# A hybrid decoder layer on one core: new homes for merged values, attention gates, turned merged tile and biases, and an earlier place in the queue for two expert half-matrices

## The chip, the cores and the metric

One core of a Trainium2 chip runs the whole layer as one program. The metric is the device time of the program in microseconds (us). The core has a matrix engine (PE, with its weight loads shown apart as PEld), a vector engine (DVE), a scalar engine (ACT), GpSimd (POOL), and SyncE (SP), which here only issues transfers. Sixteen DMA engines carry the transfers of all queues; SP's queue is q1 in the profile, POOL's is q0.

## The reference, cut to what matters

```python
# mixer: all from one input projection of the normalised x
o = diff_attention(q, k, v, lam)                   # branch A, 8 heads
y_attn = (rmsnorm(o, g_subln) * 0.8) @ w_b_attn
y_pool = multiscale_pool(u_pool, ...) @ w_b_pool   # branch B
y_mem = memory_cross_attention(...) @ w_b_mem      # branch C
g = sigmoid(gate_logits + b_gates)                 # three gates of 1024 channels
merged = g[0] * y_attn + g[1] * y_pool + g[2] * y_mem
h = x + merged @ w_out
# channel sub-layer: top 4 of 32 experts, 256 tokens, widths 1024
logits = rmsnorm(h) @ w_router + b_router
for e in experts:                                  # 12 MB of float32 weights each
    g = min(xb @ w_gate[e] + b_gate[e], 7); u = clip(xb @ w_up[e] + b_up[e], -7, 7)
    out = (g * sigmoid(1.702 * g) * (u + 1)) @ w_down[e] + b_down[e]
    y[rows] += out * weights
```

## The kernel before

**The mixer.** All mixer weights are cut into 22 pieces (`PIECES`), each loaded in two halves of 1 MB. `load(H)` issues half H on SP's queue into buffer `raw[H % 5]` once half H-5 has been used. ACT makes its high part (`hi`, L693), DVE the low part (`lo_whole`, L973), and PE multiplies (`unit`, L1483, 24 matmuls of 128x512 in a unit, or 12 for the pool and memory branches). Units are numbered: 20 to 23 are the pool branch's gates, 24 to 27 that branch, 28 to 35 the memory branch, 36 to 39 the attention gates (`ga0`, `ga1`), 40 to 43 the attention branch's product (`wba0`, `wba1`), 44 to 47 the output projection (`wo0`, `wo1`). Unit u writes PSUM bank u % 3, so unit u + 3 waits until DVE has read it. While units 21 to 36 run, PE interleaves the attention heads between them: for head h the turned q and k (`turn_qk`, semaphore `qk_done`), the scores, the turned probabilities, the values (`values`, L1626 to L1628, semaphore `pv_done`) and the turned output (`turn_o`, L1637, semaphore `oT_done`).

**Gates.** For a gate unit DVE adds the bias (`add_bias`, L1166), which POOL's queue has loaded as a broadcast 512 KB tile for each of two token tiles (`gate_bias`, L615), and ACT applies a tanh (`gate_exp`, L704). `merge` (L1185, L1190) multiplies each branch by its gate and sums into `MG`; the semaphore `merged` counts the sums, four of them for the memory branch. After the last sum PE turns `MG`, ACT and DVE split it into `MGT` high and low, and units 44 to 47 use it.

**Routing.** `add_h` (L1277) adds the projection to x. PE turns h (L1688), computes logits (L1693), DVE routes (L1291 to L1307, L1333, L1351), PE dispatches tokens (L1701), and the experts begin (L1773).

**The experts.** 16 pairs of experts, each with 12 half-matrices of 2 MB ("halves" below; 24 MB for a pair). They stream on SP's queue through a ring of 10 places of 2 MB. Half g goes to place g % 10. The ring lies over the mixer's buffers: place 0 over the attention scratch, 1 over `region9` and `mem_low`, 2 over `x_low` and `region7`, 3 over `hi4` and `raw4`, 4 over `region2` and `region8`, 5 to 8 over the other `hi` and `raw` buffers, 9 over `region1` and `region10`. So each of the first ten halves can only be issued when its place's mixer tenants are dead. SP issues in the order of its program; a wait in that program holds back all that stands behind it. Halves 10 to 17 are issued in quarters of 1 MB as PE uses up the first places (L550, L553), later ones in pieces of 2 or 4 MB.

```python
buffers = ("region9", "mem_low", "x_low", "region7", "hi4", "raw4", "region2", "region8", ...,
           "hi3", "raw3", "region1", "region10", "region0", "region5", "region3", "region4", "region6")
G = {"p": rows(6, "t"), "m": rows(7, "t"), "a": rows(6, "t")};  MG = rows(8, "t")
MGT = (rows_r(10), rows_r(1), None)
```

So `MG` sits in place 4, `MGT` in place 9, and the attention gates take the room of the pool gates.

## Time and profile before

| what | us |
|---|---|
| median of 3 runs (1213.93 to 1214.83) | 1213.95 |
| the profiled execution | 1214.63 |
| its span in the trace | 1212.8 |
| PE busy / DVE busy / ACT busy / POOL busy | 1169.5 / 436.5 / 260.5 / 43.7 |
| first expert matmul (L1773) | at 302.39 |
| granted PE clock, mean | 0.99 |

A row of the trace gives a start, a duration, the engine, the source line, the operation and its operands, and, in brackets, the idle time before it with what ended it. Transfers show two times: the issue on the queue, and the time from issue to landing.

### The profile page before, as it was taken

To read this page: it belongs to the slowest core of one execution; us is meant where nothing else is said; L and a number is where in the kernel's file an instruction comes from. 1 tells how busy PE (TensorE), PEld (TensorE's weight loads), DVE (VectorE), ACT (ScalarE), POOL (GpSimd) and SP (SyncE) were. 2 spreads that over 40 slices of the span, in tenths; PEclk is the share of its full clock that TensorE was granted. 3 is DMA by queue.
4 is the path that set the end of the run, shared out by engine and by line. 5 is a ranking of instruction groups with operands and counts; after the bars stand their busy time and mean duration, and the time that the engine had idled before them with its cause. 6 is when DMAs were issued, how large, how long until landed. Compare 5 with 4: busy or idle time off the path is not lost.

```text
span 1212.8 us, 13717 instructions
## 1 busy us (share of the span) xinstructions
PE 1169.5 (96%) x5436; PEld 581.0 (48%) x5436; DVE 436.5 (36%) x758; ACT 260.5 (21%) x463; POOL 43.7 (4%) x72
## 2 busy tenths in 40 slices
PE   9999999999999999999999999989898989899998
PEld 5888888888434344342434343433333343433342
DVE  5788798665222222222222121212122222221222
ACT  5655477542110110111010001101010101010101
POOL 1321101100000000000000000000000000000000
PEclk9999999999999999999999999999999999999999
DMA  9745645689999999999999999999999999999995
GB/s 384 267 148 185 214 142 186 224 363 394 406 427 431 427 432 432 431 432 431 430 431 430 429 429 432 431 432 431 431 431 432 432 432 431 431 431 431 425 428 232
DMA packets 28172, 460.67 MB, mean 380 GB/s; under 512 B 3216, under 2 KB 3984, under 8 KB 6608
## 3 DMA queue, kind: packets, MB, share of 16 engines
q1 hardware_dynamic: 27008, 456.34, 89.4%
q0 software_dynamic: 960, 3.41, 0.9%
q8 instruction: 49, 0.80, 0.3%
q14 instruction: 11, 0.09, 0.0%
q10 hardware_dynamic: 144, 0.03, 0.0%
HBM read 458.72 MB, written 1.05 MB: 379 GB/s over the span
## 4 chain that ended last, share of the span: by engine, by line
PE 66%; DMA 32%; issue 1%; DVE 1%; POOL 0%; SPq 0%; DVEq 0%; POOLq 0%
DMA experts_ring<-in_w_up 32%; PE bank L1773 25%; PE bank L1483 19%; PE bank L1818 7%; PE bank L1701 5%; PE bank L1761 2%; PE bank L1783 2%; PE bank L1447 1%; PE bank L1476 1%; PE bank L1784 1%; DMA raw<-in_mixer_halves 0%; PE bank L1847 0%; PE bank L1693 0%; PE bank L1602 0%; PE bank L1798 0%
## 5 line engine op out<-in xcount | busy, mean ns | idle before, releaser
L1773 PE MATMUL bank<-experts_ring,region 128*64 128x512 f32 x2048 | 468.4, 608 | 31.9 <-DMA experts_ring<-in_w_gate 21.2
L1773 PEld LDWEIGHTS bank<-experts_ring,region 128*64 128x64 f32 x2048 | 150.2, 139 | 325.5 <-issue 317.5
L1818 PE MATMUL bank<-experts_ring,region 128*64 128x512 f32 x1024 | 228.7, 596 | 2.1 <-DMA experts_ring<-in_w_down 1.9
L1483 PE MATMUL bank<-hi_split,region_split 128*128 128x512 f32 x400 | 151.3, 401 | 0.0
L1818 PEld LDWEIGHTS bank<-experts_ring,region 128*64 128x64 f32 x1024 | 73.6, 137 | 137.6 <-issue 136.4
L1483 PE MATMUL bank<-raw_split,region_split 128*128 128x512 f32 x336 | 130.9, 389 | 0.0
L944 ACT ACTIVATE region<-region 128x512 f32<-128x512 f32 x32 | 20.1, 629 | 452.3 <-DVE region L1409 452.3
L973 DVE TENSOR_TENSOR raw_split<-raw,hi_split 128x2048 fp32r<-128x2048 f32 x42 | 96.1, 2288 | 33.9 <-ACT hi_split L693 33.7
L1417 DVE TENSOR_SCALAR region<-bank 128x512 f32<-128x512 f32 x32 | 22.1, 692 | 236.7 <-PE bank L1784 236.7
L1409 DVE TENSOR_SCALAR region<-bank 128x512 f32<-128x512 f32 x32 | 22.1, 691 | 226.3 <-PE bank L1784 226.3
L1483 PEld LDWEIGHTS bank<-hi_split,region_split 128*128 128x128 f32 x400 | 75.1, 188 | 17.4 <-issue 2.6
L693 ACT ACTIVATE hi_split<-raw 128x2048 fp32r<-128x2048 f32 x42 | 80.1, 1912 | 14.7 <-DMA raw<-in_mixer_halves 14.7
L1432 DVE COPY region<-bank 64x512 f32<-64x512 f32 x32 | 22.2, 694 | 168.7 <-PE bank L1818 168.7
L1483 PE MATMUL bank<-hi_split,x_low_split 128*128 128x512 f32 x208 | 81.2, 390 | 0.0
L1483 PEld LDWEIGHTS bank<-raw_split,region_split 128*128 128x128 f32 x336 | 63.2, 188 | 12.4 <-issue 0.2
L1701 PEld LDWEIGHTS bank<-region 128*128 128x128 f32 x544 | 63.4, 192 | 2.0 <-DVE region L1333 0.5
L1701 PE MATMUL bank<-region 128*128 128x128 f32 x544 | 63.8, 275 | 0.4 <-DVE region L1333 0.4
L1761 PE MATMUL bank<-region 128*128 128x512 f32 x128 | 61.9, 606 | 0.0
L956 ACT ACTIVATE region<-bank 64x512 f32<-64x512 f32 x32 | 18.9, 590 | 152.3 <-PE bank L1818 152.3
L1392 DVE TENSOR_TENSOR region<-bank,region 128x512 f32<-128x512 f32 x68 | 43.9, 685 | 2.4 <-PE bank L1847 2.4
L1483 PEld LDWEIGHTS bank<-hi_split,x_low_split 128*128 128x128 f32 x208 | 39.0, 188 | 8.5
L1783 PEld LDWEIGHTS bank<-extra_split,region_split 128*128 128x128 f32 x64 | 11.9, 186 | 51.9 <-issue 51.9
(183 smaller groups left out, 760.2 us busy)
## 6 DMA issues: line engine op xcount, KB each, us to landing
experts_ring<-in_w_gate SPq DMA_DIRECT2D x26, 4096.0 KB, 36.6
experts_ring<-in_w_up SPq DMA_DIRECT2D x26, 4096.0 KB, 38.8
experts_ring<-in_w_down SPq DMA_DIRECT2D x26, 4096.0 KB, 39.2
raw<-in_mixer_halves SPq DMA_DIRECT2D x44, 1024.0 KB, 5.0
experts_ring<-in_w_up SPq DMA_DIRECT2D x10, 2048.0 KB, 11.1
experts_ring<-in_w_down SPq DMA_DIRECT2D x9, 2048.0 KB, 14.2
experts_ring<-in_w_gate SPq DMA_DIRECT2D x8, 2048.0 KB, 23.3
experts_ring<-in_w_gate SPq DMA_DIRECT2D x8, 1024.0 KB, 9.3
```

What stands on the lines that cost most here:

```text
L693: nc.scalar.activation(upper(H), raw(H), ACT.Copy).then_inc(hi_act, 1)
L973: nc.vector.tensor_tensor(lower(H), raw(H), upper(H), ALU.subtract).then_inc(lo_ready, 1)
L1392: nc.vector.tensor_tensor(X[:, t, h * HALF:(h + 1) * HALF], bank[banks[j]][:, :], X[:, t, h * HALF:(h + 1) * HALF], ALU.add).then_inc(y_ad ...
L1409: nc.vector.tensor_scalar(GS, bank[0][:, :], LIMIT, None, ALU.min).then_inc(g_read, 1)
L1417: nc.vector.tensor_scalar(US, bank[1][:, :], LIMIT, -LIMIT, ALU.min, ALU.max).then_inc(u_read, 1)
L1432: nc.vector.tensor_copy(OE[e * SLOTS:(e + 1) * SLOTS, HALF:D], bank[(2, 1)[e]][SLOTS:2 * SLOTS, :]).then_inc(o_hi, 1)
L1483: ins = nc.tensor.matmul(unit_bank(u)[:, :], a[:, k, toks], b[:, cols], start=(k == 0 and m == 0), stop=(k == k_n - 1 and m == 2))
L1701: ins = nc.tensor.matmul(bank[4 + half][:, b * P:(b + 1) * P], rows_[:, t, (4 * half + b) * P:(4 * half + b + 1) * P], PT[:, t, :], start= ...
L1761: nc.tensor.matmul(bank[6 + j % 2][:, :], PWT[:, t * P:(t + 1) * P], OE[:, h * HALF:(h + 1) * HALF], start=True, stop=True).then_inc(comb_ ...
L1773: ins = nc.tensor.matmul(dst[h * SLOTS:(h + 1) * SLOTS, :], XE[:, kk, e * SLOTS:(e + 1) * SLOTS], w[:, k, h * HALF:(h + 1) * HALF], start= ...
L1783: nc.tensor.matmul(dst[:, :], pick, BIAS_UP, start=False, stop=False)
L1818: ins = nc.tensor.matmul(bank[(2, 1)[e]][h * SLOTS:(h + 1) * SLOTS, :], AHT[e][:, k, half * SLOTS:(half + 1) * SLOTS], w[:, k, h * HALF:(h ...
```

## The change

Regions are given out anew. `MG` moves from `region8` to `region6` (the pool gates' own place, each value overwritten by its product); the attention gates move from `region6` to `region4`, where V is; `MGT` moves from `region10` and `region1` to `region4` and `region6`, laid out by token tile; the low part of the turned attention output moves from `region2` to `region3`, whose K is laid out by halves; `region1` and `region7` swap ring places; the expert biases go into `con`; the turned h goes to `region5`. With that, places 4 and 9 have no tenant after the last scores and the memory merge, and SP issues halves 4 and 9 there. Since V must be dead first, the attention gates' bias is now loaded after the last head's values. The router's weights and `b_down` are loaded later.

```diff
-        buffers = ("region9", "mem_low", "x_low", "region7", "hi4", "raw4", "region2", "region8", "hi0", "raw0",
-                   "hi1", "raw1", "hi2", "raw2", "hi3", "raw3", "region1", "region10",
+        buffers = ("region9", "mem_low", "x_low", "region1", "hi4", "raw4", "region2", "region8", "hi0", "raw0",
+                   "hi1", "raw1", "hi2", "raw2", "hi3", "raw3", "region7", "region10",
...
-        G = {"p": rows(6, "t"), "m": rows(7, "t"), "a": rows(6, "t")}
-        MG = rows(8, "t")
+        G = {"p": rows(6, "t"), "m": rows(7, "t"), "a": rows(4, "t")}
+        MG = rows(6, "t")
...
-        MGT = (rows_r(10), rows_r(1), None)
+        MGT = tuple(region_r[i][:, :].rearrange("p (t k n) -> p t k n", t=NT, k=KD) for i in (4, 6))
...
             for H in range(HALVES + 1, 2 * N0):
-                if H == 2 * PIECES.index("wba0") + 1:
+                load(H)
+                if H == 2 * PIECES.index("ga1"):
+                    sp.wait_ge(qk_done, HEADS)
+                    load_half(0, 4)
+                if H == 2 * PIECES.index("wba0"):
+                    sp.wait_ge(merged, 4)
+                    load_half(0, 9)
                     sp.wait_ge(pv_done, HEADS)
                     biases()
-                    sp.wait_ge(merged, 4)
                     load_half(0, 0)
-                load(H)
-                if H == 2 * PIECES.index("wba1") + 1:
+                if H == 2 * PIECES.index("wba1"):
                     sp.wait_ge(oT_done, HEADS)
                     load_half(0, 1)
-                if H == 2 * PIECES.index("wo0") + 1:
+                if H == 2 * PIECES.index("wo0"):
                     sp.wait_ge(unit_done, UNIT_OF[("ga1", NT - 1, 0)] + 1)
                     load_half(0, 2)
             sp.wait_ge(unit_done, UNIT_OF[("wba1", NT - 1, 0)] + 1)
             load_half(0, 3)
-            sp.wait_ge(mgT_done, 4)
-            load_half(0, 4)
...
             load_half(0, 8)
-            load_half(0, 9)
...
-            last = UNIT_OF[("wbp", 1, 1)]
-            pool.wait_ge(bank_read[last % 3], last // 3 + 1)
+            for h in range(3, HEADS - 1):
+                o_root(h)
+            pool.wait_ge(pv_done, HEADS)
             gate_bias(2, "a", 0)
-
-
-            for h in range(3, HEADS):
-                o_root(h)
-                if h == 5:
-                    pool.wait_ge(qk_done, HEADS)
-                    pool.dma_start(region[3][:, 1024:1280], w_router).then_inc(late_in, 16)
-            pool.wait_ge(pv_done, HEADS)
-            nc.gpsimd.memset(OE, 0.0).then_inc(seed_clear, 1)
-            pool.wait_ge(seed_clear, 1)
-            pool.dma_start(OE[0:EXPERTS, :], b_down).then_inc(seed_in, 16)
+            o_root(HEADS - 1)
+            pool.wait_ge(unit_done, UNIT_OF[("wba1", NT - 1, 0)] + 1)
+            pool.dma_start(region[3][:, 1024:1280], w_router).then_inc(late_in, 16)
...
             nc.gpsimd.memset(PWT, 0.0).then_inc(seed_clear, 1)
+            pool.wait_ge(unit_done, len(UNITS))
+            nc.gpsimd.memset(OE, 0.0).then_inc(seed_clear, 1)
+            pool.wait_ge(seed_clear, 2)
+            pool.dma_start(OE[0:EXPERTS, :], b_down).then_inc(seed_in, 16)
...
-                unit(22 + 2 * h)
+                if h + 1 < HEADS:
+                    unit(22 + 2 * h)
+                else:
+                    lo_after(36)
                 if h:
                     oT_lower(h - 1)
-            unit(37)
+            lo_after(37)
+            add_bias(36)
+            add_bias(37)
             oT_lower(HEADS - 1)
...
-            pe.wait_ge(seed_in, 16)
             pe.wait_ge(bias_lower, 1)
             def combine(it, tile):
+                pe.wait_ge(seed_in, 16)
```

The first place is SP's queue from the mixer half 34 or 35 on (`raw` is the 1 MB mixer buffer, `experts_ring` the ring). Before:

```order
L454 DMA raw<-in_mixer_halves 128x2048 [waits unit_done] x3
L496 DMA region<-in_b_gate 64x512 [waits pv_done]
L496 DMA region<-in_b_up 64x512
L488 DMA experts_ring<-in_w_gate 128x4096 [waits merged]
L454 DMA raw<-in_mixer_halves 128x2048 [waits first_half_used]
L454 DMA raw<-in_mixer_halves 128x2048 [waits unit_done]
L454 DMA raw<-in_mixer_halves 128x2048 [waits first_half_used]
L488 DMA experts_ring<-in_w_gate 128x4096 [waits oT_done]
```

And of the change:

```order
L453 DMA raw<-in_mixer_halves 128x2048 [waits unit_done]
L487 DMA experts_ring<-in_w_gate 128x4096 [waits qk_done]
L453 DMA raw<-in_mixer_halves 128x2048 [waits unit_done] x2
L487 DMA experts_ring<-in_w_down 128x4096 [waits merged]
L495 DMA con<-in_b_gate 64x512 [waits pv_done]
L495 DMA con<-in_b_up 64x512
L487 DMA experts_ring<-in_w_gate 128x4096
L453 DMA raw<-in_mixer_halves 128x2048 [waits first_half_used]
L453 DMA raw<-in_mixer_halves 128x2048 [waits unit_done]
L487 DMA experts_ring<-in_w_gate 128x4096 [waits oT_done]
```

Half 4 now stands behind mixer half 34, half 9 stands in front of the biases and half 0, and half 1 stands one mixer half earlier.

The second place is POOL, from the roots of the last heads' norms on (L586 and L588 are `inverse_root`). Before, with the gate bias standing ahead of these rows:

```order
L586 TENSOR_SCALAR stat<-stat 128x2 [waits o_squared]
L588 TENSOR_TENSOR stat<-stat,small 128x2 [waits eps_added]
L649 DMA region<-in_w_router 128x256 [waits qk_done]
L586 TENSOR_SCALAR stat<-stat 128x2 [waits o_squared]
L588 TENSOR_TENSOR stat<-stat,small 128x2 [waits eps_added]
L586 TENSOR_SCALAR stat<-stat 128x2 [waits o_squared]
L588 TENSOR_TENSOR stat<-stat,small 128x2 [waits eps_added]
L651 MEMSET region 128x1024 [waits pv_done]
L653 DMA region<-in_b_down 32x1024 [waits seed_clear]
```

And of the change:

```order
L586 TENSOR_SCALAR stat<-stat 128x2 [waits o_squared]
L588 TENSOR_TENSOR stat<-stat,small 128x2 [waits eps_added]
L615 DMA region<-in_b_gates 128x1024 [waits pv_done]
L615 DMA region<-in_b_gates 128x1024
L586 TENSOR_SCALAR stat<-stat 128x2 [waits o_squared]
L588 TENSOR_TENSOR stat<-stat,small 128x2 [waits eps_added]
L646 DMA region<-in_w_router 128x256 [waits unit_done]
```

The gate bias of the attention branch now waits for the last head's values and stands ahead of the last head's root.

The third place is DVE around the attention gates of units 36 and 37 (L973 and L972 are the low parts of mixer halves, L1229 and L1228 the low parts of turned outputs). Before:

```order
L973 TENSOR_TENSOR raw_split<-raw,hi_split 128x2048 [waits hi_act,merged]
L1166 SCALAR_TENSOR_TENSOR region<-bank,stat,region 128x512 [waits unit_done,gbias_in2]
L1229 SCALAR_TENSOR_TENSOR region_split<-bank,small,region_split 128x256 [waits oT_copied]
L973 TENSOR_TENSOR raw_split<-raw,hi_split 128x2048 [waits hi_act]
L1166 SCALAR_TENSOR_TENSOR region<-bank,stat,region 128x512 [waits unit_done,gbias_in2]
L1229 SCALAR_TENSOR_TENSOR region_split<-bank,small,region_split 128x256 [waits oT_copied]
L973 TENSOR_TENSOR raw_split<-raw,hi_split 128x2048 [waits hi_act]
```

And of the change:

```order
L972 TENSOR_TENSOR raw_split<-raw,hi_split 128x2048 [waits hi_act,merged]
L1228 SCALAR_TENSOR_TENSOR region_split<-bank,small,region_split 128x256 [waits oT_copied]
L972 TENSOR_TENSOR raw_split<-raw,hi_split 128x2048 [waits hi_act]
L1165 SCALAR_TENSOR_TENSOR region<-bank,stat,region 128x512 [waits unit_done,gbias_in2] x2
L1228 SCALAR_TENSOR_TENSOR region_split<-bank,small,region_split 128x256 [waits oT_copied]
L972 TENSOR_TENSOR raw_split<-raw,hi_split 128x2048 [waits hi_act]
```

Both bias additions now stand behind the low parts of mixer halves 35 and 36, and ahead of that of half 37.

## Rows read from the trace of the kernel before

**Rows 1.** The page: GB/s in 40 equal slices of the span.

```profile
GB/s 384 267 148 185 214 142 186 224 363 394 406 427 431 427 432 432 431 432 431 430 431 430 429 429 432 431 432 431 431 431 432 432 432 431 431 431 431 425 428 232
```

**Rows 2.** The chain that ended last: start us, length us, what.

```profile
234.31 27.23 PE bank L1483 x120
...
302.39 7.02 PE bank L1773 x32
...
329.65 1.72 PE bank L1761 x4
...
355.74 6.87 PE bank L1773 x32
...
599.57 34.18 DMA experts_ring<-in_w_up
```

**Rows 3.** Windows: busy of PE, PEld, DVE, ACT, POOL, clock, DMA share, GB/s.

```profile
200.00:220.00 20.00, 20.00 (x107) 16.23 (x104) 17.94 (x41) 15.95 (x43) 3.17 (x7) 1.00 0.46 165
220.00:240.00 20.00, 19.25 (x92) 15.75 (x91) 12.03 (x12) 8.62 (x16) 2.78 (x5) 1.00 0.63 227
```

**Rows 4.** Timeline of SP's queue, 220 to 305: start us, us, what.

```profile
228.66 0.57 SPq L496 DMA_DIRECT2D region<-in_b_gate  x1
...
229.90 0.58 SPq L488 DMA_DIRECT2D experts_ring<-in_w_gate  x1
231.40 11.46 SPq L454 DMA_DIRECT2D raw<-in_mixer_halves  x3
...
267.92 0.33 SPq L488 DMA_DIRECT2D experts_ring<-in_w_up  x1
271.55 5.82 SPq L488 DMA_DIRECT2D experts_ring<-in_w_gate  x2
...
294.73 0.80 SPq L488 DMA_DIRECT2D experts_ring<-in_w_down  x2
304.30 0.33 SPq L550 DMA_DIRECT2D experts_ring<-in_w_down  x1
```

**Rows 5.** Issues at 221.0, 267.9, 295.1, 304.3, 344.7: KB each, us to landing.

```profile
raw<-in_mixer_halves SPq DMA_DIRECT2D x1, 1024.0 KB, 4.7
...
experts_ring<-in_w_up SPq DMA_DIRECT2D x1, 2048.0 KB, 7.3
...
experts_ring<-in_w_down SPq DMA_DIRECT2D x2, 2048.0 KB, 11.6
...
experts_ring<-in_w_down SPq DMA_DIRECT2D x1, 1024.0 KB, 7.4
...
experts_ring<-in_w_up SPq DMA_DIRECT2D x1, 2048.0 KB, 9.1
```

**Rows 6.** Timelines of DVE and ACT, 224 to 246: the wait for mixer half 37.

```profile
224.47 0.69 DVE L1190 TENSOR_TENSOR region<-region,tmp 128x512 f32<-128x512 f32 x1
...
227.84 0.75 DVE L1166 SCALAR_TENSOR_TENSOR region<-bank,stat,region 128x512 f32<-128x512 f32 x1 [0.35 <-PE bank L1483]
...
241.87 1.92 ACT L693 ACTIVATE hi_split<-raw 128x2048 fp32r<-128x2048 f32 x1 [5.76 <-DMA raw<-in_mixer_halves]
...
243.82 2.29 DVE L973 TENSOR_TENSOR raw_split<-raw,hi_split 128x2048 fp32r<-128x2048 f32 x1 [7.19 <-ACT hi_split L693]
```

**Rows 7.** POOL's queue, issues at 182.6, 212.3 and 232.6: KB each, us to landing.

```profile
region<-in_b_gates POOLq DMA_DIRECT2D x2, 512.0 KB, 4.4
...
region<-in_w_router POOLq DMA_DIRECT2D x1, 128.0 KB, 2.5
...
region<-in_b_down POOLq DMA_DIRECT2D x1, 128.0 KB, 7.0
```

**Rows 8.** Routing: timelines of POOL and DVE, 230 to 304.

```profile
231.34 0.95 POOL L651 MEMSET region<- 128x1024 f32 x1
...
298.69 0.31 POOL L660 MEMSET region<- 128x256 f32 x1 [1.37 <-DVE region L1297]
...
299.53 0.54 DVE L1333 TENSOR_SCALAR region<-con,region,stat 128x64 f32<-128x64 f32 x2
```

More of the change, by code:

```diff
@@ L257, in decoder_layer @@
         MEM = rows(3, "t")
-        K = rows(3, "t")
         MEMT = (rows_r(4), LO_R, LO)
@@ L266, in k_part @@
         def k_part(t, half):
-            return K[:, t, half * HALF:(half + 1) * HALF]
+            return region[3][:, half * D + t * HALF:half * D + (t + 1) * HALF]
         def group_cols(u):
@@ L292, in decoder_layer @@
         O_JUNK = region[9][:, 1536:1664]
-        OT = (rows_r(5), rows_r(2), None)
+        OT = (rows_r(5), rows_r(3), None)
         OMT = (rows_r(10)[:, 0:4, :], LO_R[:, 4:8, :], LO[:, 4:8, :])
         Z2T = (rows_r(10)[:, 4:8, :], LO_R[:, 0:4, :], LO[:, 0:4, :])
-        MGT = (rows_r(10), rows_r(1), None)
+        MGT = tuple(region_r[i][:, :].rearrange("p (t k n) -> p t k n", t=NT, k=KD) for i in (4, 6))
         POOLW = region[10][:, 0:512].rearrange("p (g n) -> p g n", g=GROUPS)
@@ L302, in decoder_layer @@
         HN = rows(5, "t")
-        HNT = rows(6, "k")
-        H_JUNK = region[4][:, 0:1024]
+        HNT = rows(5, "k")
+        H_JUNK = region[3][:, 0:1024]
         LATE_TMP = extra[:, :]
@@ L321, in decoder_layer @@
         PWT = region[3][:, 1280:1536]
-        BIAS = region[4][:, 512:1024]
+        BIAS = con[:, C_MASK:C_ALL]
         BIAS_UP = extra_r[:, :]
@@ L869, in _ @@
                 hi_after(b)
-                gate_exp_of(b)
+                if h + 1 < HEADS:
+                    gate_exp_of(b)
                 if h:
@@ L875, in _ @@
             o_out(HEADS - 1)
+            gate_exp(36)
             gate_exp(37)
@@ L886, in mgT @@
                 h, t = divmod(j, 2)
-                nc.scalar.activation(MGT[0][:, 4 * h:4 * h + 4, t * P:(t + 1) * P],
+                nc.scalar.activation(MGT[0][:, t, 4 * h:4 * h + 4, :],
                                      bank[3 + j][:, :].rearrange("p (k n) -> p k n", k=4), ACT.Copy, scale=0.5).then_inc(mgT_copied, 1)
@@ L930, in _ @@
             act.wait_ge(gT_done, 1)
-            act.wait_ge(seed_clear, 2)
+            act.wait_ge(seed_clear, 1)
             nc.scalar.activation(PWT[0:EXPERTS, :], bank[6][0:EXPERTS, 0:SEQ], ACT.Copy).then_inc(wT_copied, 1)
@@ L1240, in _ @@
                     head_weights(h + 1)
-                unit(22 + 2 * h)
+                if h + 1 < HEADS:
+                    unit(22 + 2 * h)
+                else:
+                    lo_after(36)
                 if h:
                     oT_lower(h - 1)
-            unit(37)
+            lo_after(37)
+            add_bias(36)
+            add_bias(37)
             oT_lower(HEADS - 1)
@@ L1252, in merged_lower @@
                 h, t = divmod(j, 2)
-                at = (slice(None), slice(4 * h, 4 * h + 4), slice(t * P, (t + 1) * P))
+                at = (slice(None), t, slice(4 * h, 4 * h + 4), slice(None))
                 nc.vector.scalar_tensor_tensor(out=MGT[1][at], in0=bank[3 + j][:, :].rearrange("p (k n) -> p k n", k=4), scalar=0.5,
@@ L1307, in weigh @@
                 nc.vector.tensor_scalar(GATE[:, t, :], GATE[:, t, :], s, None, ALU.mult).then_inc(gate_ready, 1)
+            add_h(44)
+            add_h(45)
             dve.wait_ge(late_in, 16)
@@ L1471, in unit_k @@
                     toks = slice(t * P, (t + 1) * P)
+                    at = (slice(None), t, k, slice(None)) if name in ("wo0", "wo1") else (slice(None), k, toks)
                     if H < EARLY:
@@ L1482, in unit_k @@
                     for m, (a, b) in enumerate(((high, upper(H)), (high, lower(H)), (low, upper(H)))):
-                        ins = nc.tensor.matmul(unit_bank(u)[:, :], a[:, k, toks], b[:, cols],
+                        ins = nc.tensor.matmul(unit_bank(u)[:, :], a[at], b[:, cols],
                                                start=(k == 0 and m == 0), stop=(k == k_n - 1 and m == 2))
```

2 lines of the change are left out of this document (removed).

## The prediction

> **What bounds the kernel now.** I read the page first. From the ninth slice on the transfers run close to their plateau of 431 GB/s, and only the slices from 30 to 240 us lie far below it [rows 1]. At 431 GB/s an expert half of 2 MB takes 4.87 us, a mixer half of 1 MB 2.43 us. The chain that ended last shows the two regimes. From 302 to 599 us it is PE alone; at 599.57 it goes through a transfer for 34 us [rows 2], and so in each pair behind it. PE needs 355.74 - 302.39 = 53.4 us for the first pair [rows 2], the 24 MB of a pair need 12 x 4.87 = 58.4, so PE eats up the ring's lead over five pairs and then waits for the stream until the end. The stream has no slice below its plateau from about 340 to the last one [rows 1], so the end moves with the stream, one for one, and PE's own speed does not matter unless PE's use of places holds the stream back. The windows before the experts show idle DMA: a busy share of 0.46 from 200 to 220 and 0.63 from 220 to 240 [rows 3], that is 10.8 + 7.4 = 18.2 us.
>
> **What the earlier halves bring.** Halves 4 and 9 are now issued at 271.55 (the first of the two there) and at 295.1 (the second of the two from 294.73) [rows 4]. They move into the idle stretch: half 4 behind mixer half 34, as soon as the last head's q and k are turned, half 9 after the last sum of the memory merge, 224.47 + 0.69 = 225.2 [rows 6]. Both fit, 9.7 us of transfer. But the ring has only ten places, and the eleventh half needs place 0 back. Its first quarter is issued when PE has used that much, at 304.30, 1.9 us after the first expert matmul [rows 2, 4]. This row sets where the gain ends. Before, half 9 landed at 295.1 + 11.6 = 306.7, so the queue was just not empty at 304.30, and the quarter landed 7.4 later, at 311.7 [rows 5]. In the change half 8 is the last of the ten; issued at 294.73 into an empty queue it lands 7.3 later, at 302.0, and the queue then runs dry. A 1 MB transfer into an empty queue lands after 4.7 [rows 5], so the quarter lands at 309.0, not 311.7: 2.7 earlier. Of the 9.7 us moved, 7 come back as new idle time around 273 to 278 and 302 to 305, since half 5 waits for the output projection as before. A second limit lies a little later: the half issued at 344.74 landed after 9.1, against 7.3 with an almost empty queue [rows 5], so no more than 1.8 passes this point. The lower bound is 0.1: of the quarter's 4.7 only 2.43 is data, and if the other 2.3 all lies ahead of the data, these start at 306.6 whether half 9 is there or not. I take 1.6, near the upper limit, because it is by landings that PE and the places go.
>
> **What the change costs on the way.** PE runs without a pause from 234.31 through units 38 to 42, 27.23 us for 120 matmuls, 5.45 a unit [rows 2], so any stall there moves the experts' start and with it the row at 304.30.
>
> The tightest wait is that for mixer half 37, the second half of `wba0`. Its high part started at 241.87 on its landing, its low part was ready at 243.82 + 2.29 = 246.1 [rows 6]. Unit 40 needs it at 234.31 + 2.5 x 5.45 = 247.9, so there were 1.8 us to spare. Ahead of it in the change stand half 9, issued at 225.2 and landing at 225.2 + 7.3 = 232.5, then the expert biases (0.6), the gate bias (1 MB, 2.4, now in this stretch), half 0 (4.9), and itself (2.4): 242.8. The same sum for before, from the issue of half 0 at 229.90 [rows 4] with 2.3 for what is not data, gives 229.9 + 2.3 + 4.9 + 2.4 = 239.5, plus 0.3 for `b_down`, which leaves the stretch: 239.8. The difference is 3.0, less the 1.8 to spare: a stall of 1.2. Its bounds are 0 (the real landing lay 2 us above my sum for before, so the sum is rough) and 3.0. Mixer half 39 now stands behind half 1, which is issued a mixer half earlier: 242.8 + 2.4 + 4.9 + 2.4 = 252.5, and the splits take 4.2 more, 256.7; unit 42 needs it at 234.31 + 4.5 x 5.45 = 258.8. Covered by 2.1 us, and by more if PE is late.
>
> The attention gates' bias is now issued at about 228.7, where SP's biases show the last values done [rows 4]. It was landed long before the addition at 227.84 [rows 6]. Unit 39 needs bank 0, which this addition (0.75) sets free, at 234.31 + 5.45 = 239.8, so the bias must land by 239.0. In an empty queue it takes 4.4 [rows 7] after the second issue at 229.3: 233.7. Under the stream the same 128 KB took 7.0 instead of 2.5 [rows 7], 4.5 more: 238.2. That is 0.8 in time, so I cost it at nothing, but its cover is thin (first rival). The two issues, 0.6 each, stand ahead of the last head's root on POOL; what that root leads to, the last turned output, is wanted by PE only at 234, behind unit 37. DVE keeps the low parts of halves 35 and 36 ahead of the additions, so PE's next units are not held by them.
>
> The cleared seed tile (0.95 on POOL, [rows 8]) moves from 231 into the routing, behind the clearing at 298.69, so it runs at 299.0 to 300.0 beside the slot rows of DVE at 299.53 [rows 8], which are on the path. Nothing in this trace has the two side by side; the price is between 0 and 0.95, and I take 0.2, as the operations share no data. `b_down` then lands near 308; its first reader is the combine at 329.65 [rows 2], 20 us later. `w_router` is issued when half 3 is, at 267.9, lands by 275 even if it takes 7.0, and is read behind the first additions, not before 271.55 + 5.82 = 277.4, when PE is halfway through unit 45 [rows 4]. Layouts, the order of the router's products behind the first additions, and the repeated wait on the seed cost nothing: PE is continuous there on other work, and from 600 on it waits for the stream.
>
> **Sum.** 1214.63 - 1.6 + 1.2 + 0.2 = 1214.4 against the profiled execution, which stood 0.7 above the median of 1213.95. So 1213.8 as a median: no change that a measurement can tell (about 0.2%, 2.4 us).
>
> **The rivals.**
>
> *The gate bias comes late* (the other side, slower). It is decided at a landing of 239.0. If each DMA engine serves the two queues piece by piece, the bias's sixteen pieces of 4 KB an engine wait for the eight pieces of half 0 and the eight of mixer half 37: all three end together, 232.5 + 4.9 + 2.4 + 2.4 = 242.2, a stall of 3.2 for unit 39, which hides the one for half 37. The time is 1213.95 - 1.6 + 3.2 + 0.2 = 1215.8; if both bias transfers suffer `b_down`'s 4.5 in turn, 242.7, and with the queue's own 2.3 on top a stall of up to 6.0, 1218.6. For it speaks that 128 KB lost 4.5 us under load; against it that 4.5 is just what was left of half 0 when `b_down` was issued at 232.6 (by the sum above half 0 lands at 229.9 + 2.3 + 4.9 = 237.1), so that it may have waited for one transfer and not for each piece.
>
> The Trainium skill bears on this, in DMA: Bandwidth & Descriptors, section "Queues, rings and completion order": an engine goes round the queues and drains a whole packet of typically 9 to 17 descriptors before it turns to the next. By that rule each bias transfer would wait for at most one expert half, and the likeliest case would stand; the trace's `b_down` at 7.0 agrees, but it is one small transfer and not proof.
>
> *Nothing is delayed.* Half 37 lands by 243.6, inside its 1.8: 1213.95 - 1.8 = 1212.2, with the stream's gain at its limit.
>
> *The whole 9.7 is gained*, 1204.3. It would need the stream to go on without a pause from 302 to 305, thus an eleventh place or a first use earlier than 304.30. Nothing in the diff moves the experts' start forward.
>
> *The change does nothing at all*: the start of the stream is set by the issue at 304.30 and the gain is at its bound of 0.1. With the same stall, 1213.95 - 0.1 + 1.4 = 1215.3.
>
> **How the numbers follow.** Likeliest case (gain 1.6, stall 1.2, both within their bounds, 1212.4 to 1215.4): 0.40. Nothing delayed: 0.15. No gain: 0.10. Late bias: 0.26, half of it beyond 1216.4. The whole gain or another large one: 0.06. The rest, 0.03, is a stall that I don't see. Faster by over 0.2%: the 0.06 and a tail of 0.04 of the second case, 0.10. Slower: 0.13 + 0.03 and tails of 0.06, 0.22. Within: 0.68. The range of eight in ten reaches from the nothing-delayed case at its best, 1212.0, into the late bias, 1217.6.
>
> **What would show it.** In the new profile: DMA share near 1 from 208 to 216 and from 226 on, and a gap of some 2 to 4 us before the first quarter; that quarter landing in about 5 us, not 7.4; ACT's high part of half 37 starting near 245, and PE waiting about 1 us in unit 40; the gate addition of unit 36 done before 239.8. It is wrong if PE waits ahead of unit 39 for that addition, if the first expert matmul is not within 0 to 3 us of 302.4, or if the first quarter is issued earlier than 304.

## The result, and the profile of the changed kernel

The changed kernel takes 1221.38 us as a median of 4 runs (1221.02 to 1223.28), the kernel before in the same comparison 1214.39 (1213.93 to 1215.11). The ratio is 1.006, with a 95% interval of 1.0043 to 1.0078: slower by 7.0 us, outside the range of the forecast. The profiled execution took 1221.02, its span is 1219.1 (before 1212.8).

I looked for the place where the two traces part. First the chain that ended last: start, length, what.

```profile
228.76 0.29 issue
229.05 0.60 POOL region L615
...
229.65 14.07 DMA region<-in_b_gates
...
243.74 0.76 DVE region L1165
...
244.55 24.34 PE bank L1488 x96
...
309.72 7.02 PE bank L1778 x32
...
605.94 35.20 DMA experts_ring<-in_w_up
```

In [rows 2] the same stretch was PE alone. Now the chain leaves PE at 228.76, stays 14.07 us in the transfer of the attention gates' bias, and comes back to PE at 244.55. The first expert matmul starts at 309.72, not 302.39: 7.33 later. The row behind 600 us has moved by 6.4 and the span by 6.3, so what was lost here is kept nearly whole until the end. The next view is the engines at that place: start, length, engine, line, and in brackets the idle time and what ended it.

```profile
229.05 1.13 POOL L615 DMA_DIRECT2D region<-in_b_gates  x2 [8.58 <-PE bank L1633]
243.74 1.41 DVE L1165 SCALAR_TENSOR_TENSOR region<-bank,stat,region 128x512 f32<-128x512 f32 x2 [10.06 <-DMA region<-in_b_gates]
244.55 0.79 PE L1488 MATMUL bank<-hi_split,region_split 128*128 128x512 f32 x1 [4.64 <-DVE region L1165]
245.14 0.63 PE L1488 MATMUL bank<-raw_split,region_split 128*128 128x512 f32 x1
```

Unit 39 waits 4.64 us for bank 0, which the addition of unit 36 frees, which waits for the bias. The matmuls then come 0.42 apart, where those of unit 38 came 0.23 apart. The windows say why (columns as in [rows 3]; the sixth figure is the granted clock).

```profile
200.00:220.00 20.00, 20.00 (x108) 16.22 (x105) 17.96 (x41) 15.86 (x43) 2.52 (x6) 1.00 0.69 263
220.00:240.00 20.00, 19.17 (x90) 15.32 (x89) 10.24 (x9) 7.39 (x13) 2.54 (x5) 1.00 0.83 307
240.00:242.00 2.00, 0.00 (x0) 0.00 (x0) 0.00 (x0) 0.00 (x0) 0.00 (x0) 1.00 0.98 410
242.00:244.00 2.00, 0.00 (x0) 0.00 (x0) 0.26 (x1) 0.00 (x0) 0.00 (x0) 0.66 0.99 414
246.00:248.00 2.00, 2.00 (x6) 1.61 (x5) 0.48 (x1) 1.98 (x2) 0.00 (x0) 0.50 1.00 426
248.00:250.00 2.00, 2.00 (x7) 1.51 (x7) 1.99 (x1) 0.00 (x0) 0.00 (x0) 0.64 1.10 467
250.00:252.00 2.00, 2.00 (x11) 1.65 (x10) 0.96 (x2) 1.00 (x2) 0.00 (x0) 1.00 0.78 250
```

While PE stood idle its granted clock fell to half, the 1.2 GHz level, and from 250 on it was back at the full one. So units 39 to 42 took 24.34 us instead of 4 x 5.45 = 21.8: another 2.6. Pause and clock together are 4.64 + 2.6 = 7.2 of the 7.33. Everything behind them kept its length.

The DMA share shows that the halves did move: 0.69 and 0.83 where [rows 3] has 0.46 and 0.63. Last, the start of the ring's second round, in SP's queue, and what that quarter took to land:

```profile
311.63 0.33 SPq L550 DMA_DIRECT2D experts_ring<-in_w_down  x1
```

```profile
experts_ring<-in_w_down SPq DMA_DIRECT2D x1, 1024.0 KB, 4.9
```

Before, it was issued at 304.30 and landed after 7.4 [rows 4, 5]. The 2.5 us of the forecast are there, and still the end has moved by nearly as much as the issue.

### The profile page after: what moved, and what is told of

Same layout as the page of the kernel before. It is cut to its first block, busy times and chain, and to the rows that moved or that the text cites. A ratio compares the mean times of both kernels' runs of the same rounds, so it can differ in the third digit from the quotient of the medians.

```text
span 1219.1 us, 13746 instructions
## 1 busy us (share of the span) xinstructions
PE 1171.8 (96%) x5436; PEld 582.3 (48%) x5436; DVE 436.7 (36%) x758; ACT 260.9 (21%) x463; POOL 43.9 (4%) x72
## 4 chain that ended last, share of the span: by engine, by line
PE 64%; DMA 34%; DVE 1%; issue 1%; POOL 0%; ACT 0%; SPq 0%; DVEq 0%; POOLq 0%
DMA experts_ring<-in_w_up 29%; PE bank L1778 25%; PE bank L1488 17%; PE bank L1823 7%; PE bank L1706 5%; DMA experts_ring<-in_w_gate 3%; PE bank L1766 2%; PE bank L1788 2%; PE bank L1451 1%; DMA region<-in_b_gates 1%; PE bank L1481 1%; PE bank L1789 1%; PE bank L1497 1%; DMA raw<-in_mixer_halves 0%; DVE raw_split L972 0%
## 5 line engine op out<-in xcount | busy, mean ns | idle before, releaser
L1421 DVE TENSOR_SCALAR region<-bank 128x512 f32<-128x512 f32 x32 | 22.2, 692 | 239.6 <-PE bank L1789 239.6
L972 DVE TENSOR_TENSOR raw_split<-raw,hi_split 128x2048 fp32r<-128x2048 f32 x42 | 96.1, 2289 | 29.0 <-ACT hi_split L690 28.8
```

The costliest lines, as they stand in the source:

```text
L972: nc.vector.tensor_tensor(lower(H), raw(H), upper(H), ALU.subtract).then_inc(lo_ready, 1)
L1421: nc.vector.tensor_scalar(US, bank[1][:, :], LIMIT, -LIMIT, ALU.min, ALU.max).then_inc(u_read, 1)
```

## The experiments

In the table "refill" is the issue of the first quarter that reuses a place (304.30 before), with its shift, and "median" the time against that of the kernel before on the same chip. The refill is read in one profiled execution, the median over 4 to 11; the profiled one lay within 0.9 us of its median, except in sp_bias (1.5 above), fix_bothlate (1.75) and pool_half0_late (2.6).

| label | refill | shift | median | ratio, 95% |
|---|---|---|---|---|
| the change | 311.63 | +7.3 | +7.0 | 1.0060 [1.0043, 1.0078] |
| sp_bias | 308.05 | +3.8 | +3.5 | 1.0027 [1.0018, 1.0036] |
| act_bias | 306.59 | +2.3 | +2.9 | 1.0022 [1.0013, 1.0031] |
| late_only | 307.16 | +2.9 | +2.6 | 1.0023 [1.0014, 1.0032] |
| no9 | 305.32 | +1.0 | +1.1 | 1.0006 [0.9997, 1.0016] |
| warm | 308.60 | +4.3 | +5.1 | 1.0044 [1.0028, 1.0059] |
| fix_4late | 306.12 | +1.8 | +2.5 | 1.0022 [1.0012, 1.0031] |
| fix_9late | 305.38 | +1.1 | +0.8 | 1.0009 [1.0000, 1.0018] |
| fix_bothlate | 305.91 | +1.6 | +1.3 | 1.0013 [1.0004, 1.0022] |
| best | 305.40 | +1.1 | +1.7 | 1.0011 [1.0002, 1.0020] |
| best_bothlate | 304.89 | +0.6 | +0.7 | 1.0002 [0.9993, 1.0011] |
| best_fine | 306.00 | +1.7 | +0.8 | 0.9999 [0.9990, 1.0008] |
| pool_half0_late | 305.57 | +1.3 | +1.6 | 1.0010 [1.0001, 1.0019] |
| final | 304.93 | +0.6 | +0.6 | 1.0007 [0.9998, 1.0016] |
| final_bothlate | 304.63 | +0.3 | +0.4 | 1.0002 [0.9993, 1.0011] |
| final_fine | 304.80 | +0.5 | -0.4 | 0.9997 [0.9988, 1.0006] |
| before_fine | 304.51 | +0.2 | -0.6 | 0.9995 [0.9986, 1.0004] |
| final_fine_bothlate | 304.50 | +0.2 | +0.7 | 1.0007 [0.9998, 1.0016] |

### Which part makes the bias late

**sp_bias**: the change, with the gate bias on SP's queue instead of POOL's, behind half 9 and ahead of the expert biases.

```diff
 # SP, at mixer half wba0, behind half 9
                     sp.wait_ge(pv_done, HEADS)
+                    for t in range(NT):
+                        sp.dma_start(G["a"][:, t, :], b_gates[0:D]...).then_inc(gbias_in[2], 16)
                     biases()
                     load_half(0, 0)
 # POOL
-            pool.wait_ge(pv_done, HEADS)
-            gate_bias(2, "a", 0)
             o_root(HEADS - 1)
```

> The changed kernel with one edit: the attention gates' bias (2 x 512 KB) is issued on SP's queue, behind the wait for the last values and ahead of the expert biases, instead of on POOL's queue. Theory A (the two queues share the DMA engines piece by piece, so that the bias on POOL's queue is starved by half 9, half 0 and mixer half 37): in one queue the bias lands by 236 to 238, the addition of unit 36 is done before 239.8, PE does not wait at unit 39 and its clock stays at 1.00; the experts start at 302.4 to 303.5, and the whole is 0.5 to 1.5 us under the kernel before (1213 us), so 7 to 8 under the changed kernel. Theory B (the ring's two early halves load the stream so much that PE waits anyway, for mixer half 37 or the splits behind it): the stall moves to unit 40 and 2 us or more of the 7 stay.

**act_bias**: the same two transfers on ACT's queue, ahead of the last head's squares.

```diff
+            act.wait_ge(pv_done, HEADS)
+            for t in range(NT):
+                act.dma_start(G["a"][:, t, :], b_gates[0:D]...).then_inc(gbias_in[2], 16)
             o_squares(HEADS - 1)
```

> The changed kernel with one edit: the same bias transfers issued on ACT's queue, a hardware queue of its own, at the same point. Theory A (two queues share piece by piece, whichever the second is): the bias lands at 240 to 244, PE waits 2 to 5 us at unit 39, time within 2 us of the changed kernel (1219 to 1222). Theory C (POOL's software queue itself is the slow part, by its start under load): the bias lands by 237, no stall at unit 39, about 1213 to 1214.

**late_only**: the kernel before, with nothing but its gate bias moved behind the last values, and the order of DVE and ACT that goes with it.

```diff
 # POOL
-            gate_bias(2, "a", 0)
             for h in range(3, HEADS):
+                if h == HEADS - 1:
+                    pool.wait_ge(pv_done, HEADS)
+                    gate_bias(2, "a", 0)
                 o_root(h)
 # DVE, at the last head: lo_after(36), lo_after(37), and only then
+            add_bias(36)
+            add_bias(37)
```

> The kernel before with one part of the change: the attention gates' bias is loaded only after the last values, with the order of POOL, DVE and ACT around it as in the change; all homes and SP's queue as before, so half 9 is not in front. Theory A: the bias shares with the expert biases, half 0 and mixer half 37 alone and lands at 239 to 241.5; PE waits 0.3 to 3 us at unit 39; 0 to 5 us over the kernel before, the more if the clock falls. Theory D (half 9 is the cause): landing by 237, no stall, same as before within 0.5 us. Theory C: landing at 243 to 244 as in the changed kernel, 7 us over.

**no9**: the change, with half 9 back behind half 8.

```diff
                     sp.wait_ge(merged, 4)
-                    load_half(0, 9)
...
             load_half(0, 8)
+            load_half(0, 9)
```

> The changed kernel with half 9 issued last, behind half 8, as before the change; half 4 stays early, the bias stays on POOL's queue. Theory A: the bias lands 2 to 4 us earlier than in the changed kernel (240 to 242), the stall at unit 39 shrinks from 4.6 to 1 to 3 us. The gain at the ring's first refill is lost, since the queue is not empty then: the end moves with the experts' start, 1 to 6 us over the kernel before.

The addition that waits for the bias, in sp_bias, act_bias, late_only and no9 in that order (one fence each):

```profile
235.59 1.41 DVE L1166 SCALAR_TENSOR_TENSOR region<-bank,stat,region 128x512 f32<-128x512 f32 x2 [2.30 <-DMA region<-in_b_gates]
```

```profile
240.19 1.41 DVE L1167 SCALAR_TENSOR_TENSOR region<-bank,stat,region 128x512 f32<-128x512 f32 x2 [5.96 <-DMA region<-in_b_gates]
```

```profile
237.00 1.41 DVE L1166 SCALAR_TENSOR_TENSOR region<-bank,stat,region 128x512 f32<-128x512 f32 x2 [3.48 <-DMA region<-in_b_gates]
```

```profile
236.15 1.41 DVE L1165 SCALAR_TENSOR_TENSOR region<-bank,stat,region 128x512 f32<-128x512 f32 x2 [2.86 <-DMA region<-in_b_gates]
```

A bias as late as in the change needs both a queue of its own and half 9 standing in SP's queue. On SP's queue the addition starts at 235.6 even behind half 9; on POOL's without half 9 at 236.2; on POOL's with it at 243.7. ACT's queue, 240.2, is on the late side too (PE waits 1.46 at unit 39), so it is not POOL's alone. So the bias loses by sharing with another queue. Not all of this was expected. Theory A had the bias at 239 to 241.5 in late_only and at 240 to 242 in no9, where it came at 237.0 and 236.2: beside half 0 alone it is not late. Sp_bias, expected 0.5 to 1.5 us under the kernel before, is 3.5 over it: there theory B came true, a stall that moves to unit 40. Act_bias has the landing of theory A, but with +2.9 not its time. How the two share is seen in the queues' own rows of the changed kernel, from 232 to 235 and from 235 to 242 us (packets, MB, share of the 16 engines; q0 is POOL's, q1 SP's):

```profile
q0 software_dynamic: 160, 0.62, 68.6%
q1 hardware_dynamic: 147, 0.28, 30.3%
...
q1 hardware_dynamic: 199, 2.44, 84.5%
q0 software_dynamic: 124, 0.42, 15.7%
```

Taken over stretches of some us, the two queues here move packets of like number: 160 to 147 in the first, 95 to 115 from 235 to 240; after 240 the bias runs out on one engine after the other, which makes it 124 to 199 for the whole of the second. In the first, SP's queue holds the expert biases, in small packets, and POOL's queue has most of the time. In the second it holds expert half 0, whose packets are four times as large as the bias's, and nearly all of the last 0.42 MB of the bias takes 7 us at a share of 15.7%.

What half 9 does is seen in no9, from 231 to 233 and from 233 to 235:

```profile
q0 software_dynamic: 120, 0.44, 103.7%
q1 hardware_dynamic: 11, 0.02, 2.9%
...
q0 software_dynamic: 112, 0.40, 66.1%
q1 hardware_dynamic: 76, 0.28, 40.8%
```

There the first packet of the bias moves 1.7 us after its issue, and by 235 only 11 of its 288 are left. In the change it moves 3.1 us after its issue, at 232.2, when the large packets of half 9 are through. So half 9 costs the bias its place beside the small packets of the expert biases, and the rest of it meets half 0. The queues do not take single packets in turn: in no9 POOL's queue moves 105 packets from 230.75 to 232.0 and SP's none, though SP issued its second expert bias at 229.07 and its first, issued at 228.45, was moving 1.6 us later. In late_only it is 82 to none from 230.75 to 231.75. So a turn is longer than one packet. In none of the three that have it early (sp_bias, late_only, no9) does PE pause ahead of unit 39.

But none is as fast as before, and late_only, which has neither early half, still loses 2.6 us. Its trace shows the next wait in line, the one that I had priced at 1.2: mixer half 37 (ACT's high part, and PE at unit 40).

```profile
246.15 1.92 ACT L691 ACTIVATE hi_split<-raw 128x2048 fp32r<-128x2048 f32 x1 [6.71 <-DMA raw<-in_mixer_halves]
...
250.45 0.50 PE L1488 MATMUL bank<-hi_split,region_split 128*128 128x512 f32 x1 [2.55 <-DVE raw_split L973]
```

In the kernel before this half landed at 241.87 [rows 6]. The later bias alone, 1 MB in this stretch, moved it by 4.3 us and made PE wait 2.55. So the bias's new home costs about as much in late_only as the early halves were ever to bring, whether or not the bias itself is late. In no9 the pause is 0.9, in sp_bias 2.1.

**pool_half0_late**: the change (bias on POOL's queue), with ring half 0 behind mixer halves 37 and 38.

```diff
                     biases()
-                    load_half(0, 0)
...
                 if H == 2 * PIECES.index("wba1"):
+                    load_half(0, 0)
                     sp.wait_ge(oT_done, HEADS)
```

> The changed kernel with the bias left on POOL's queue, and ring half 0 issued behind mixer halves 37 and 38. Theory A (piecewise sharing with the large pieces of half 0 starves the bias, which shares only with 8 KB pieces of the mixer halves here and with the end of half 9): the bias lands at 236 to 238.5, no pause at unit 39, a pause of 0 to 1 us at unit 40; time within 1.5 us of the kernel before. If half 9 alone starves it: landing at 241 or later and 3 to 7 us over.

```profile
238.88 1.41 DVE L1165 SCALAR_TENSOR_TENSOR region<-bank,stat,region 128x512 f32<-128x512 f32 x2 [5.54 <-DMA region<-in_b_gates]
```

Still 3.3 later than in sp_bias, but the first of the two additions ends at 239.6, just ahead of unit 39, so no pause there; the only one is 0.8 at unit 42. Half 9 stands ahead as in the change, and with half 0 moved away the bias is 4.9 earlier: it takes both halves of 2 MB to make it as late as 243.7.

### What the clock cost

**warm**: the change, with five fp32 matmuls between units 38 and 39 whose results nothing reads. They are work added to the kernel, to keep PE busy while the bias is on its way.

```diff
             unit(38)
+            for _ in range(5):
+                nc.tensor.matmul(bank[3][:, :], ident, X[:, 0, 0:HALF], start=True, stop=True)
             unit(39)
```

> The changed kernel with five float32 matmuls of 128x512 put between units 38 and 39, into a PSUM bank whose content nobody reads, so that PE works on through the wait for unit 39 (it adds work and takes none away; the output is the same). Theory E (the pause of 4.6 us lets the granted clock fall, and the half clock from 243 to 249 costs another 2.7 us): unit 39 starts at 244.5 to 245 as before, the clock stays at 1.00, and the experts start 2 to 2.7 us earlier than in the changed kernel (307.0 to 307.7), the whole 2 to 2.7 us faster (1218.7 to 1219.4). Rival F (the 2.7 us are something else, such as later landings of mixer halves 39 to 41): the experts start at 309.7 again, 1221.4.

PE's rows and the window:

```profile
239.29 4.45 PE L1669 MATMUL bank<-region,con 128*128 128x512 f32 x10
...
243.80 0.50 PE L1488 MATMUL bank<-hi_split,region_split 128*128 128x512 f32 x1
```

```profile
240.00:244.00 4.00, 3.95 (x10) 1.53 (x9) 1.01 (x2) 0.23 (x1) 0.00 (x0) 1.00 0.97 403
```

And from the chain that ended last, units 39 to 42 and the first expert matmul:

```profile
243.80 22.06 PE bank L1488 x96
...
306.69 7.02 PE bank L1780 x32
```

Unit 39 still has to wait for the bias, to 243.80, the clock stays at 1.00, and the experts start at 306.7 instead of 309.7. Of these 3.0 us, 0.75 come from a bias that landed that much earlier; the other 2.3 are the clock: the same 96 matmuls take 22.06 instead of 24.34. From the change I had read 2.6. The median gives 1.9 back (+5.1 against +7.0), less than the shift of 3.0, within what the two intervals leave open; the four times of warm (1219.6 to 1219.9) all lie below the four of the change (1221.0 to 1223.3). So the clock's part is real and of about this size; the pause is the larger part.

### Where the ring's gain goes

**fix_4late, fix_9late, fix_bothlate**: sp_bias with half 4, half 9, or both at the places that they had before.

```diff
-                    load_half(0, 4)          # behind mixer half 34
...
             load_half(0, 3)
+            sp.wait_ge(mgT_done, 4)
+            load_half(0, 4)
...
             load_half(0, 8)
+            load_half(0, 9)                  # from ahead of the biases
```

> The bias on SP's queue as in sp_bias, and both ring halves 4 and 9 issued where they were before the change. This is the new homes without the new transfers. Theory G (the ring's gain is fixed by whether the queue is empty at the first refill): as the kernel before, 1214 us, and 1 us over sp_bias. Theory H (each early half brings some gain by itself): also about 1214, so this run only sets the zero.

> The bias on SP's queue as in sp_bias, half 4 early, half 9 last. Theory G: the queue is not empty at the first refill, which then lands in 6.5 to 7.4 us; no gain, the same as fix_bothlate within 0.3 us. Theory H: half of sp_bias's gain, 0.5 us under fix_bothlate.

> The bias on SP's queue as in sp_bias, half 9 early, half 4 late. Theory G: half 8 is the last of the ten and the first refill lands in 5 us; the whole gain of sp_bias, about 1 us under fix_bothlate. Theory H: half of it.

All were expected at about 1214 or under it, and stand 0.8 to 2.5 us over the kernel before: PE still waits for mixer half 37, 1.1 us in fix_bothlate, 1.0 in fix_9late, 1.6 in fix_4late. Theory G had fix_4late 1 us under fix_bothlate; it stands 1.2 over. Half 9 late makes half 37 land at 244.4 instead of 245.5. The start moves with it, and the time with the start. Beyond that nothing is seen: sp_bias, with both halves early, stands 0.29 below its own shift, fix_bothlate, with neither, 0.26 below.

**best, best_bothlate, best_fine**: best is sp_bias with ring half 0 behind mixer halves 37 and 38 (the edit of pool_half0_late); best_bothlate has halves 4 and 9 late besides; best_fine has the refills of the first pair in quarters to the tenth step, not the eighth.

```diff
-IN_STEPS = 8
+IN_STEPS = 10
...
+                            if g < IN_STEPS and k == 1:
+                                ins.then_inc(quarter_used, 1)
                         ins.then_inc(used, 1)
```

> The changed kernel with the gate bias on SP's queue (as in sp_bias) and ring half 0 issued behind mixer halves 37 and 38 instead of ahead of them; halves 4 and 9 early. Theory A completed (both new waits come from what stands in front of the gate bias and of mixer half 37): half 37 lands by 239, PE has no pause at unit 39 or 40, the first expert matmul is at 302.3 to 302.7 and the first refill is issued at 304.3 to 304.6. Then the end tells the worth of the early halves alone. Theory G (the refill meets an empty queue): 0.5 to 1.6 us under the kernel before. Theory I (the end follows the issue of the first refill, and the queue's state then is worth nothing): the same as before within 0.3 us.

> The same with halves 4 and 9 issued as late as before the change. Same first expert matmul (302.3 to 302.7). Theory G: 0.5 to 1.6 us over the kernel best, level with the kernel before. Theory I: no difference to best.

> The kernel best with ten instead of eight of the refilled halves issued in quarters of 1 MB (places 8 and 9 as well), so that the refills behind 344 are issued up to 2 us earlier. Theory J (what the queue gains at the first refill is lost again at 344.7, where it runs short of issued work): 0.5 to 2 us under best. If the end follows the first refill alone: no difference to best.

Half 37 lands at 240.5 and neither unit 39 nor unit 40 waits. Now mixer half 39, behind ring half 1, is late (ACT, in best):

```profile
255.33 1.92 ACT L691 ACTIVATE hi_split<-raw 128x2048 fp32r<-128x2048 f32 x1 [3.77 <-DMA raw<-in_mixer_halves]
```

PE waits 0.8 for it in best, 0.55 in best_bothlate, 1.6 in best_fine. The stall that I had called covered appears once nothing ahead of it delays PE, with the same transfers in front of it in the queue, half 0 nearer to it.

**final, final_bothlate, final_fine, before_fine, final_fine_bothlate**: final is best with ring half 1 behind mixer half 39. The others add both halves late, the fine refills, or both; before_fine is the kernel before with the fine refills.

```diff
                     load_half(0, 0)
-                    sp.wait_ge(oT_done, HEADS)
-                    load_half(0, 1)
+                if H == 2 * PIECES.index("wba1") + 1:
+                    sp.wait_ge(oT_done, HEADS)
+                    load_half(0, 1)
```

> The kernel best with ring half 1 moved behind mixer half 39 as well, so that half 39 has only half 0 in front. Then no wait is left: first expert matmul at 302.2 to 302.6, first refill issued at 304.2 to 304.6. Halves 4 and 9 early. If the early halves are worth nothing: the same as the kernel before within 0.5 us. If their worth (0.5 to 1.6 us) was only hidden by the pause of best: 1213 to 1214, 0.5 to 1.6 under before.

> The same with halves 4 and 9 late: the zero for final. Same first refill. The same as the kernel before within 0.5 us; final lies 0 (worth nothing) or 0.5 to 1.6 (theory G) under it.

> final with ten refilled halves in quarters instead of eight. Theory J (the queue's gain at the first refill is lost at the refills behind 344): 0.7 to 2 us under final and under before. Otherwise the same as final.

> The kernel before with ten refilled halves in quarters and nothing else. If the 1.0 us between final and final_fine needs the empty queue of the early halves: the same as before within 0.4 us. If the finer refill is worth it by itself: 0.5 to 1.5 us under before.

> final_fine with halves 4 and 9 late. If the early halves bring their gain once the refills are finer: 0.5 to 1.5 us over final_fine, at 1215 to 1215.5. If not: level with final_fine at 1214.3.

Final has no pause of PE above 0.4 us, and both early halves. It should show the ring's gain if there is one. It stands 0.6 above before, just its shift of the refill, and final_bothlate, without the early halves, 0.4. Over the eight kernels with both or only half 9 early and coarse refills, the median's shift less that of the refill is +0.3 on the mean (from -0.3 to +0.8); over the six with half 9 late it is -0.1 (from -0.3 to +0.1). A gain would be a lower number in the first group. There is none. Nor is there one if the profiled executions are compared with each other instead of the medians: time less shift is then +0.7 and +0.5 on the mean of the two groups.

Landing times of the same transfers, counted from the refill's issue, show it going (KB and us to landing in the rows). In the change the issue at +0 took 4.9, above, and that at +40.4 (352.07):

```profile
experts_ring<-in_w_up SPq DMA_DIRECT2D x1, 2048.0 KB, 8.1
```

| issue after the refill | before | change | final | final_bothlate |
|---|---|---|---|---|
| +0 | 7.4 | 4.9 | 4.8 | 9.1 |
| +40.4 | 9.1 | 8.1 | 7.9 | 10.8 |
| +44.6 | 9.8 | 9.5 | 9.2 | 11.5 |
| +66.7 | 17.2 | 17.0 | 17.7 | 18.7 |
| +97.8 | 16.2 | 16.4 | 17.1 | 17.1 |

Against before, the stream's lead is 2.5 us at the first refill, 1.0 to 1.2 at +40, and 0.2 or less than nothing 26 us on. Final_bothlate is the better zero for final, as it differs by the two halves alone, and there the lead is larger: 4.3 at the refill, 2.9 at +40, 1.0 at +66.7. At +97.8 it is gone as well. Counted from the refill, every issue up to +264 falls at the same time within 0.1 us in these four kernels, however early or late the transfers land: up to there the issues follow PE, which gives the places back, and not the stream. And at several of them the queue is nearly empty (landings of 8 to 9, against 17 later, where the pieces are 4 MB), so that the next transfer starts when its place comes back, whatever was loaded earlier. So the gain is lost at the places, not at the refill alone. Which issue takes how much of it was not tested.

The fine refills were the test whether more frequent places keep it. Final_fine stands at -0.4, its twin without the early halves at +0.7, before_fine at -0.6, all with 1 in their intervals. The 1.1 between the first two has the sign of a kept gain; that before_fine does as well without any early half speaks against it. Best_fine is 0.9 under best with a start 0.6 later. So three of the four fine kernels lie 0.8 to 0.9 below their shift, with early halves or without, and the fourth 0.5 above; the finer refills may be worth something by themselves. This stays open: differences of 1 us are at the limit of what these runs tell apart. No version is shown to beat the kernel before.

## Why the prediction was wrong

**The step that failed** is the one on the gate bias: "That is 0.8 in time, so I cost it at nothing, but its cover is thin (first rival)". The bias was to land at 238.2; it landed at 243.7. I had priced load on the second queue by one row, the 4.5 us that 128 KB lost, and added it once for both transfers of the bias. The first of the two took 8.7 us and the second 14.1, against 4.4 at the median without load [rows 7]: 4.3 and 9.7 more, near to 4.87, one expert half, for the first and twice that for the second. The bytes agree: between the second issue and the last landing SP's queue moved 4.28 MB, two halves' worth, 0.85 of it before the bias's first packet. The rival had the wait, and for its cause a sharing by pieces, which the runs do not show (next paragraph); its price was 3.2 for the stall, up to 6.0 if each of the two transfers suffers in turn; measured are 4.64. My reason against it, that the 4.5 might be a wait for one transfer and not for each piece, fits the traces better, but was no reason against a late bias: two transfers that wait once each come as late. But once for each is no general price. Without half 9, with half 0 in SP's queue all the same, the two took 5.9 us at the median (no9), only 1.5 more than without load; that one half more then moves the addition by 7.6, over 4.87, because it pushes the bias from beside the small packets to beside the large ones.

The Trainium skill's rule, in DMA: Bandwidth & Descriptors, section "Queues, rings and completion order", has an engine drain a whole packet of one queue before it turns to the next. I had written that by it "each bias transfer would wait for at most one expert half, and the likeliest case would stand". The rule was not what failed, but the second half of my sentence: an estimate worked out for two transfers that each wait for one half gives 229.3 + 4.4 + 2 x 4.87 = 243.4, a stall of 4.4, and the bias was there at 243.7. This was added up after the result, and the same sum would put the bias of no9 and of late_only, with half 0 in the queue there too, later than it came. The traces bear the rule out against single packets in turn: the runs of 105 and 82 packets of one queue, above, and the bias's first packet, which moves only at 232.2, once half 9 is through, where without half 9 it moved 1.7 us after the issue. How many packets an engine takes in one turn no run shows, since the rows don't part the 16 engines.

**The clock** was not in the sum or in any rival. It made the stall of 4.64 cost 7.2. Without it the result would lie at about 1218.8, by the rival's highest price of 1218.6, which still had the 1.6 of the ring in it. The clock page of the Trainium skill (TensorE: Matmul & The Clock Gate, Part 1) has TensorE come out of idleness at 1.2 GHz, and the trace of the change agrees, with 0.50 behind the pause; after shorter pauses not every kernel does (last section).

**The ring's gain, "I take 1.6"**, was right at the first landing (2.5 us, forecast 2.7) and at the second limit (1.0 for "no more than 1.8"), and wrong in its end: I took landings at 344.7 for the time at the end, but the lead is used up behind that point, by +97.8 after the refill even against final_bothlate. The profiled execution of the change still gives 1.0 back between the start of the experts (+7.3) and the end (+6.3), but its median only 0.3 (+7.0), and the other kernels nothing; my bound below, 0.1, lies nearest. That the whole 9.7 us cannot be had was right.

**Mixer half 37, "a stall of 1.2"**: the mechanism was right, the size within its bounds. In the change the bias's pause hides it; without that pause PE waits 2.1 (sp_bias), 2.55 (late_only) or 0.9 (no9). The largest term of that sum was the 2.4 of the gate bias, and late_only bears it out and more: the bias alone moves half 37 by 4.3.

**Mixer half 39, "Covered by 2.1 us"**: true in the change, where PE is 7 us late, but not in best, where PE is on time and it costs 0.8. **The seed tile**, 0.2: nothing. From 278.86 to 309.72 the change takes as long, 30.86, as before from 271.52 to 302.39, 30.87. `w_router`, `b_down` and the repeated waits: nothing, as said.

## What to carry to other kernels

A small late transfer on its own queue beside a stream of large ones is not priced by its time alone, but by what the other queue moves meanwhile: here from 1.5 us beside small packets to one large transfer for each of its own. Put it on the stream's queue ahead of what it must beat, or keep its old early place. Price a stall of TensorE with what its clock does afterwards, and list not only the wait that ends last but the next two in line; here each fix uncovered the next one. And bytes that are moved to an idle stretch ahead of a ring bring nothing if later issues find the queue empty and wait for places: look for the last such issue and count the gain there.

## What the runs showed of the hardware that was not expected

Equal numbers, unequal bytes. The bias is 4 KB a partition and transfer (1024 f32), an expert half 16 KB (2 MB over 128 partitions). Beside half 0 the two queues moved like numbers of packets (95 to 115 from 235 to 240), so the one with the smaller packets had 0.33 of 2.06 MB there; but in turns of many packets, not of one (105 to none for 1.25 us in no9). ACT's queue was not spared: 8.7 us at the median of the two transfers, against 11.4 on POOL's and 4.4 alone.

The clock after short pauses. It fell to 0.50 in the change after a pause of 4.64 us, and also in sp_bias, where no single pause was longer than 2.1:

```profile
250.00:252.00 2.00, 2.00 (x7) 1.54 (x7) 0.38 (x1) 1.58 (x2) 0.00 (x0) 0.64 0.94 393
252.00:254.00 2.00, 2.00 (x6) 1.53 (x5) 1.12 (x1) 0.84 (x1) 0.00 (x0) 0.51 0.99 414
```

In late_only it stayed at 1.00 through a pause of 2.55:

```profile
250.00:252.00 2.00, 1.55 (x7) 1.29 (x8) 1.05 (x2) 0.91 (x2) 0.00 (x0) 1.00 0.97 414
```

So a pause's length alone does not tell whether the clock falls. What does, these runs leave open.
